# Values and keys by token between the products of the inverse's levels: a recurrent mixer's solve on one core

## What is computed

```python
def step(state, inp):
    r_t, w_t, k_t, v_t, a_t, b_t = inp
    sa = jnp.einsum('bhvk,bhk->bhv', state, a_t)
    state = state * w_t[:, :, None, :] + sa[..., None] * b_t[:, :, None, :] + v_t[..., None] * k_t[:, :, None, :]
    return state, jnp.einsum('bhvk,bhk->bhv', state, r_t)
```

## Time and profile before

| what | value |
|---|---|
| median of three runs | 2957.77 us (2954.75 to 2964.93) |
| the profiled execution, its own time | 2960.55 us |
| its span | 2958.4 us |
| PE busy | 2899.7 us, 98% |
| VectorE, ScalarE, GpSimd busy | 53%, 38%, 43% |
| granted TensorE clock, mean | 0.996 |
| DMA | 282 MB, mean 95 GB/s |

### The profile page before, as it was taken

The page is one execution under the profiler, slowest core; times in us unless marked ns, Lnnn a source line. Parts: engine busy times, 40 slices in busy tenths (PEclk is TensorE's granted clock), DMA queues, the critical chain, the costliest instruction groups (busy, mean ns, idle before and its releaser), DMA issues. The chain is left out here.

```text
span 2958.4 us, 62088 instructions
## 1 busy us (share of the span) xinstructions
PE 2899.7 (98%) x27008; PEld 2391.0 (81%) x27008; DVE 1553.5 (53%) x1823; ACT 1111.3 (38%) x1841; POOL 1275.2 (43%) x674
## 2 busy tenths in 40 slices
PE   8999999999999999999999999999999999999998
PEld 6888888888788888878888888877778888888887
DVE  7644444543366565656666666355336744443443
ACT  5333334333334443434444344433233433334342
POOL 2544446362455545445455554222130444445451
PEclk9999999999999999999999999999999999999999
DMA  6222236344321111131112112351023222225442
GB/s 195 98 75 78 82 114 238 110 146 164 96 68 57 51 51 50 40 117 51 50 50 65 55 53 84 113 178 56 29 70 122 93 86 86 82 90 193 161 151 63
DMA packets 286314, 282.04 MB, mean 95 GB/s; under 512 B 14176, under 2 KB 236640, under 8 KB 284896
## 3 DMA queue, kind: packets, MB, share of 16 engines
q1 hardware_dynamic: 286048, 278.12, 29.2%
HBM read 227.75 MB, written 50.33 MB: 94 GB/s over the span
## 5 line engine op out<-in xcount | busy, mean ns | idle before, releaser
L1713 POOL TENSOR_TENSOR panels_low<-arena,panels_high 128x1024 fp32r<-128x1024 f32 x103 | 256.4, 2490 | 359.7 <-ACT panels_high L2120 352.3
L671 POOL TENSOR_TENSOR panels_low<-arena,panels_high 128x1024 fp32r<-128x1024 f32 x97 | 241.9, 2495 | 327.6 <-ACT panels_high L855 327.6
L1825 PE MATMUL bank<-half_high,panels_high 128*128 128x512 f32 (+1 forms) x896 | 355.9, 397 | 8.1 <-DMA half_low<-h_spill 5.2
L1825 PE MATMUL bank<-half_low,panels_high 128*128 128x512 f32 (+1 forms) x896 | 341.1, 381 | 0.0
L1825 PE MATMUL bank<-half_high,panels_low 128*128 128x512 f32 (+1 forms) x896 | 339.5, 379 | 0.8 <-issue 0.8
L1825 PEld LDWEIGHTS bank<-half_high,panels_high 128*128 128x128 f32 x896 | 169.4, 189 | 59.4 <-issue 16.7
L1966 PE MATMUL bank<-arena 64*64 64x64 f32 x5120 | 205.9, 225 | 4.1 <-issue 1.6
L771 PE MATMUL bank<-h_high,panels_high 128*128 128x512 f32 x528 | 205.4, 389 | 0.0
L771 PE MATMUL bank<-h_low,panels_high 128*128 128x512 f32 x528 | 205.4, 389 | 0.0
L771 PE MATMUL bank<-h_high,panels_low 128*128 128x512 f32 x528 | 205.4, 389 | 0.0
L1067 DVE TENSOR_TENSOR ffn_work<-bank,ffn_work 128x512 f32<-128x512 f32 x80 | 54.9, 688 | 280.1 <-ACT ffn_work L914 190.2
(11 more groups left out here) (407 smaller groups left out, 7629.3 us busy)
## 6 DMA issues: line engine op xcount, KB each, us to landing
arena<-w_in SPq DMA_DIRECT2D x96, 512.0 KB, 3.8
arena<-w_down SPq DMA_DIRECT2D x88, 512.0 KB, 4.1
a_spill<-ffn_work SPq DMA_DIRECT2D x88, 256.0 KB, 2.1
arena<-a_spill SPq DMA_DIRECT2D x88, 256.0 KB, 2.7
arena<-w_gate SPq DMA_DIRECT2D x19, 1024.0 KB, 5.5
arena<-w_up SPq DMA_DIRECT2D x19, 1024.0 KB, 8.0
arena<-w_ckv SPq DMA_DIRECT2D x16, 512.0 KB, 4.4
bridge<-w_out SPq DMA_DIRECT2D x14, 512.0 KB, 5.0
```

The source lines that it names most:

```text
L671: nc.gpsimd.tensor_tensor(low, src, high.bitcast(F32), ALU.subtract).then_inc(s_low, 1)
L1713: G.tensor_tensor(pw[1][:, unit % 2], raw[unit % 2], pw[0][:, unit % 2].bitcast(F32), ALU.subtract).then_inc(S("panel_low"), 1)
L1825: last = mm(dst, pw[wp][:, unit % 2, kt], src, start=term == 0, stop=term == TERMS - 1)
```

## The change

Slots 6 and 7 go (SCORES falls from 8 to 6), and the chain begins two slots sooner as well (FIRST_CHAIN from 4 to 2), so that it meets the levels as before. The 16 calls of `heads` that made values and keys by token are issued between the `to_other` products of four parts: values of chunks 0 to 3 in part (1,0), 4 to 7 in (2,1), keys in (3,0) and (3,1). They go to the bank of the projections that is not in use there (`token_bank`). ScalarE stores them in the slots of parts (2,2) and (3,2). The waits that slots 6 and 7 had move to part (0,2). On GpSimd, `next_panel(i, 4)` moves from the end of `prepare` to a place behind `x0_ready` in `solve`.

```diff
--- before.py
+++ after.py
@@ -1587,10 +1587,15 @@
...
             ZB, TB, XB = (F2, F3), F0, F1
-            SCORES, FIRST_CHAIN = 8, 4
+            SCORES, FIRST_CHAIN = 6, 2
             SLOTS = SCORES + 4 * len(LEVELS)
...
             TERMS = 3 * KT
+
+            TOKENS = {(1, 0): ("v", 0), (2, 1): ("v", 4), (3, 0): ("k", 0), (3, 1): ("k", 4)}
+
+            def token_bank(i):
+                return P0 if inside(i)[0] % 2 else P1
 
...
@@ -1765,8 +1770,10 @@
...
                             root_var()
-                        for j in range(2, NP - 1):
+                        for j in range(2, NP - 2):
                             next_panel(i, j)
+                        if not live:
+                            next_panel(i, NP - 2)
 
...
@@ -1988,18 +1996,15 @@
...
                                 scores(F3, k_ch, 0).then_inc(S("k_scores_ready"), 1)
-                            elif s == 5:
+                            else:
                                 pe.wait_ge(S("proj_stored"), stored(i, 0))
                                 scores(P0, k_ch, 1).then_inc(S("k_scores_ready"), 1)
-                            elif s == 6:
-                                seen("n_stored")
-                                seen("n_copied")
-                                by_heads(F0, lambda n: vm[:, n * CH:(n + 1) * CH], lambda n: c("stack_ident"),
-                                         every).then_inc(S("v_tok_ready"), 1)
-                            else:
-                                seen("base_stored", 2, 1)
-                                by_heads(F1, lambda n: k_ch[:, n, :], lambda n: cur[:, n, 2, :],
-                                         every).then_inc(S("k_tok_ready"), 1)
+
+                        def token_product(name, n):
+                            out = one(token_bank(i))[:, n, :]
+                            if name == "v":
+                                return heads(out, vm[:, n * CH:(n + 1) * CH], c("stack_ident"))
+                            return heads(out, k_ch[:, n, :], cur[:, n, 2, :])
 
...
@@ -2014,18 +2019,31 @@
...
                                     seen("xt_added", 10, 2 * n - 1 + q)
+                                tokens, first = TOKENS.get((n, k), (None, 0))
+                                if tokens == "v" and first == 0:
+                                    if token_bank(i) == P0:
+                                        seen("before_stored", 2, 2)
+                                    else:
+                                        seen("b_tok_stored")
+                                elif tokens == "k" and first == 0:
+                                    seen("v_tok_stored")
                                 for m, at in enumerate(chunks):
...
                                         last.then_inc(S("z_ready"), 1)
+                                    if tokens:
+                                        last = token_product(tokens, first + m)
+                                        if first + m == NC - 1:
+                                            last.then_inc(S(f"{tokens}_tok_ready"), 1)
                                     if beside and m > 0:
...
                                     seen("x0_ready")
-                                    seen("v_tok_stored")
-                                    seen("k_tok_stored")
+                                    seen("n_stored")
+                                    seen("n_copied")
+                                    seen("base_stored", 2, 1)
                                 else:
...
@@ -2224,12 +2242,12 @@
...
                                 A(flat(b_tok[i % 2]), bank[:, P1, :], ACT.Copy).then_inc(S("b_tok_stored"), 1)
-                            elif live and s == 6:
+                            elif live and s == SCORES + 10:
                                 seen("v_tok_ready")
-                                A(flat(v_tok[i % 2]), bank[:, F0, :], ACT.Copy).then_inc(S("v_tok_stored"), 1)
-                            elif live and s == 7:
+                                A(flat(v_tok[i % 2]), bank[:, token_bank(i), :], ACT.Copy).then_inc(S("v_tok_stored"), 1)
+                            elif live and s == SCORES + 14:
                                 seen("k_tok_ready")
-                                A(flat(k_tok[i % 2]), bank[:, F1, :], ACT.Copy).then_inc(S("k_tok_stored"), 1)
+                                A(flat(k_tok[i % 2]), bank[:, token_bank(i), :], ACT.Copy).then_inc(S("k_tok_stored"), 1)
                             if back and s >= FIRST_CHAIN:
...
```

## The result

The change takes 2964.69 us (median of 13 runs, 2957.86 to 2968.34), the kernel before in the same comparison 2960.48 us (13 runs): ratio 1.0016, 95% interval 1.0009 to 1.0023. That is 4 us more where 19 us less were forecast. The profiled execution took 2968.34 us, its span is 2966.2. It is the longest of the 13, and 4.5 of the 7.8 us by which its span exceeds that of the kernel before arise ahead of the first slot 0, which starts at 830.55 us and not at 826.04.

A forecast was written before the change was run, and what follows sets the result against it. TensorE, busy 98% of the span, was taken as the bound. Per chained step 1.86 - 0.70 + 0.26 - 0.27 = 1.15 us, times 15, plus 1.5 in the first, gave 18.8 us: from 2957.77 to 2939 us, range 2929 to 2949.

The forecast's parts named there:

- A shift without cause in the step: Rival: the 30.8 us part varies between steps where instructions come late; a few us either way, no separate chance given.
- The sum: All terms per chained step, 1.15 us in 15 steps, and 1.5 us in the first: 18.8 us less.
- Early part of the step: Start of the step, chain begun two slots sooner: late operands make PE wait, 0.27 us charged, bounds 0 and 0.6.
- ScalarE's store of keys: ScalarE's store no longer delays the chain's next store, for which PE waits: 0.26 us gained in 15 steps.
- Two slots against six pairs that stick out: Slots 6 and 7 going saves 1.86 us a step; six token pairs not hidden in four parts cost 0.70.
- the kinds do not overlap: Rival: beside the chain, `heads` and `to_other` products do not overlap, 16 pairs cost 1.87 us; about 2958 us, chance 0.10.
- The slower rival: GpSimd's moved panel subtraction blocks VectorE's second identity addition: about 20 us lost, 2978 us, chance 0.05.
- The sign I had named for this rival: In the profile after, the panel's subtraction itself taking over 2.5 us would make the slower rival true.
- The panel itself is for the next step's first unit, 20 us off, and SP's load behind it ... nothing.: Moved panel subtraction and SP's load, asked for 3.6 us later: margin enough, so no cost.
- First step: First step, without a chain: 1.86 us saved less 0.3 for level 1's late mask, 1.5 us gained.

The follow-up runs named there:

- late_load: The change with SP's load of the next panel held back until the step's last Z product; 2958.51 us, ratio 0.9984 to the kernel before.
- shift_64: The change with 128 long-satisfied waits added once ahead of the mixer, counted as 63 more instructions; 2958.50 us, ratio 0.9995 to the kernel before.

## Why the prediction was wrong

The step that failed is the one put as "A shift without cause in the step": the part of 30.8 us "varies by some tenths to a microsecond between steps where instructions come late; a few us either way". Late instructions had a cause, and the edit fed it. The sum priced the array's time and waits for other engines only. It took the earlier trace rows for the proof that one pair of each kind runs in 0.117 us, which is true, and did not ask how long TensorE could be fed at 15.3 ns a record: there it was 64 records, which with their weight loads are half a block. What it called noise was 6.7 us, and became 27.3. The gap between forecast and result is 23 us: 20.6 are new issue waits, 1.2 a gain smaller than the sum, and the rest is no more than the granted clock can be (1 to 2 us).

The other steps, by the rows:

- *Early part of the step, forecast 1.86 less with 0.27 charged for late operands.* Right. Step 9 after, timelines of PE, VectorE and GpSimd:

```profile
1446.23 0.27 PE L1815 MATMUL bank<-mix_work 64*64 64x64 f32 x2
...
1452.27 0.33 PE L1815 MATMUL bank<-mix_work,arena 64*64 64x64 f32 x4
...
1452.68 0.27 PE L1974 MATMUL bank<-arena 64*64 64x64 f32 x2
```

```profile
1449.03 0.82 DVE L2480 TENSOR_TENSOR arena<-arena 128x256 f32<-128x256 f32 x1
...
1450.48 0.78 DVE L2480 TENSOR_TENSOR arena<-arena 128x256 f32<-128x256 f32 x1
...
1451.94 0.27 DVE L2513 SCALAR_TENSOR_TENSOR mix_work<-mix_work,bank 128x64 f32<-128x64 f32 x1
```

```profile
1448.48 1.09 POOL L1780 TENSOR_TENSOR arena<-arena 128x512 f32<-128x512 f32 x1 [6.02 <-ACT arena L2238]
1449.65 1.33 POOL L1783 TENSOR_TENSOR arena<-arena 128x512 f32<-128x512 f32 x1
1450.94 2.54 POOL L1718 TENSOR_TENSOR panels_low<-arena,panels_high 128x1024 fp32r<-128x1024 f32 x1
```

  Level 0's first `to_other` record stands 1452.68 - 1446.23 = 6.45 us into the step. Before, it is a row that the earlier trace rows leave out:

```profile
1448.10 0.27 PE L1966 MATMUL bank<-arena 64*64 64x64 f32 x2
```

  That is 8.22 us into the step: 1.77 less, where 1.86 - 0.27 = 1.59 was forecast. PE reaches chunk 1's first link 6.04 us in (forecast 6.0), and the state of chunk 0 is done at 5.98 (forecast 6.2), since both identity additions end a little sooner than I took, the second at 5.03 instead of 5.3.
- *ScalarE's store of keys.* Right: the 15 waits for L2237, 2.5 us in the view, are gone.
- *Two slots against six pairs that stick out.* The sum came out well: 17.6 us won without the issue waits, against 18.8. Part (1,0) in step 9, the tokens' products (`arena,mix_work`) beside the inverse's, shows both kinds in step, some 58 ns for two records of each:

```profile
1457.01 0.23 PE L1815 MATMUL bank<-arena,mix_work 64*64 64x64 f32 x2
1457.03 0.22 PE L1974 MATMUL bank<-arena 64*64 64x64 f32 x2
1457.07 0.22 PE L1815 MATMUL bank<-arena,mix_work 64*64 64x64 f32 x2
1457.08 0.22 PE L1974 MATMUL bank<-arena 64*64 64x64 f32 x2
```

  The rival "the kinds do not overlap" is false here as well. The rule of the Trainium skill in TensorEngine Tiling (section Restrictions and Gotchas), that row tiles may not be in one PSUM bank at a time, does not show as time in these rows either.
- *The slower rival, VectorE shut out by the panel.* False: the second L2480 began at 1450.48, under GpSimd's L1783, and ended at 1451.26, 0.28 us after L1783 (1450.98), as its like did before; the panel, whose row starts at 1450.94, did not hold it up. It took 0.78 us, where the shortest of the earlier trace rows took 0.60. The sign I had named for this rival was a bad one: the panel did take over 2.5 us (2.54). The Trainium skill's SBUF — State Buffer (section SBUF: two separate sides) says that the shared port pair goes to whichever instruction starts first; here that was again the one that had been waiting, ahead of GpSimd's next.
- *"The panel itself is for the next step's first unit, 20 us off, and SP's load behind it ... nothing."* Wrong, and the second failure. The load had time enough for its own user; what it collided with was the fetch of instructions. late_load prices it at 6 to 9 us.
- *First step, forecast 1.5 less.* 2.2 us more; its issue waits are 3.4 us, and in shift_64, without them, it was 1.9 us shorter than before (23.1 against 25.0 us from slot 0 to the inverse's last product).

What stays open: why a block is often asked for only a microsecond or more after the one ahead is entered, and why an added wait costs 28 ns between dense parts, 11 ns in the preparation, and far more in the row of 256 ahead of the mixer. Nor does any run take all the new waits away and keep the gain, so their 20.6 us are read from the waits views, and the runs show the part of it that they moved.

## What to carry to other kernels

Where a stream of small matmuls is made denser, count its instructions (weight loads and waits too) against the rate at which they are fetched, not only its time in the array: here a block of 256 seldom lasted under 3.3 us, and 4.0 to 4.4 us in step 5, where PE waited for each. Waits for "issue" that recur in the profile before can be that rate's mark, so price what they become when the same instructions get less time. And a transfer that is moved with an engine's work can cost through what it delays, here instruction fetches.

## What the runs showed of the hardware

TensorE's program is fetched in packets of 16 KB, 256 instructions, as it runs (213 packets for 54016 matmuls and weight loads). In the mixer a packet took 0.9 to 1.5 us, over 2 in single cases (2.3 in shift_64). Away from long matmuls it starts no sooner than 0.5 us before the block ahead is entered, mostly 0.2 to 2.1 us after; where long matmuls run, it can start some us earlier (up to 5.1 in the change). Beside a 512 KB load it starts later (2.6 us in the median of nine cases, 1.15 without), and PE enters the block no sooner than 1.2 us after the packet has landed. Dead instructions ahead of a loop moved the loop's time by 5 to 6 us (63 or 127 of them), but 127 cost as much where they stood: PE stood still for 9.80 us, and the granted clock was at 1.2 GHz for 10.2 us. A satisfied wait is not free on TensorE: 11 ns each ahead of 128x512 matmuls in the preparation.
